# Sixteen more tokens fetch their rows of the first expert table; the high product of the one-hot gates moves to ScalarE

## What is computed

```python
def peer_ffn(xn, w_query, sub_keys, u, v):     # T = 512 tokens, H = 8 heads, K = 16 of 128 x 128 experts each
    q = (xt @ w_query).reshape(T, H, 2, PEER_HALF)
    s = jnp.einsum('thpd,hpkd->thpk', q, sub_keys)
    top_s, top_i = lax.top_k(s, K)
    cand_s = (top_s[:, :, 0, :, None] + top_s[:, :, 1, None, :]).reshape(T, H, K * K)
    cand_i = (top_i[:, :, 0, :, None] * PEER_KEYS + top_i[:, :, 1, None, :]).reshape(T, H, K * K)
    best_s, best_pos = lax.top_k(cand_s, K)
    expert_idx = jnp.take_along_axis(cand_i, best_pos, axis=-1)
    gate = jax.nn.softmax(best_s, axis=-1)
    ...
        act = jnp.einsum('td,ted->te', x_blk, u[i_blk])
        hid = jax.nn.gelu(act, approximate=False) * g_blk
        return jnp.einsum('te,ted->td', hid, v[i_blk])
```

## Time and profile before

| | us |
|---|---|
| median of 3 runs | 2528.64 (2528.29 to 2529.47) |
| the profiled execution | 2528.59 |
| its span in the trace | 2526.8 |
| PE busy | 2516.0 |
| DVE busy | 1609.6 |
| ACT busy | 1035.0 |
| POOL busy | 1001.8 |

### The profile page before, as it was taken

One profiled execution on the slowest core, in us unless ns is written; L12 is line 12 of the kernel. 1 busy time (PEld: TensorE's weight loads), 2 busy tenths in 40 slices (PEclk: granted clock), 3 DMA queues, 4 the chain that ended last, 5 costly groups with the idle time before them and its releaser, 6 DMA issues.

```text
span 2526.8 us, 35751 instructions
## 1 busy us (share of the span) xinstructions
PE 2516.0 (100%) x13652; PEld 2191.4 (87%) x13652; DVE 1609.6 (64%) x3032; ACT 1035.0 (41%) x1624; POOL 1001.8 (40%) x548
## 2 busy tenths in 40 slices
PE   9999999999999999999999999999999999999999
PEld 7789899999999988888888888888889877988888
DVE  5746989899999978888888656610216275730112
ACT  6634344444444433333333534522324365532332
POOL 3323344545555523333332044444442424254442
PEclk9999999999999999999999999999999999999999
DMA  4413255689999999999999332223322322232231
GB/s 139 142 59 119 90 156 163 216 286 372 390 397 397 327 328 339 360 349 352 354 347 342 128 117 84 92 96 97 100 93 75 125 84 74 69 117 94 99 100 59
DMA packets 193482, 488.08 MB, mean 193 GB/s; under 512 B 18560, under 2 KB 84256, under 8 KB 193056
## 3 DMA queue, kind: packets, MB, share of 16 engines
q1 hardware_dynamic: 156304, 351.49, 41.5%
q0 software_dynamic: 36864, 134.23, 14.2%
q10 hardware_dynamic: 144, 0.07, 0.0%
HBM read 442.71 MB, written 42.88 MB: 192 GB/s over the span
## 4 chain that ended last, share of the span: by engine, by line
PE 95%; ACT 1%; DVE 1%; POOL 1%; DMA 1%; issue 0%; SPq 0%; ACTq 0%; DVEq 0%; POOLq 0%
PE ps L314 30%; PE ps L316 30%; PE ps L315 30%; PE ps L1817 2%; PE ps L2838 1%; PE ps L2935 1%; PE ps L1627 1%; PE ps L2898 1%; POOL wl L303 1%; DMA wraw<-in_w_in 1%; PE ps L528 0%; ACT wh L295 0%; POOL Xl L587 0%; PE ps L2323 0%; DVE tmpb L1204 0%
## 5 line engine op out<-in xcount | busy, mean ns | idle before, releaser
L295 ACT ACTIVATE wh<-wraw 128x1024 fp32r<-128x1024 f32 x483 | 509.8, 1059 | 1178.7 <-PE ps L316 1165.3
L303 POOL TENSOR_TENSOR wl<-wraw,wh 128x1024 fp32r<-128x1024 f32 x252 | 615.0, 2447 | 929.5 <-ACT wh L295 819.2
L314 PE MATMUL ps<-Xh,wh 128*128 128x512 f32 (+2 forms) x2328 | 826.3, 355 | 2.7 <-DVE wl L1309 0.8
L316 PE MATMUL ps<-Xh,wl 128*128 128x512 f32 (+2 forms) x2328 | 814.5, 350 | 0.0
L315 PE MATMUL ps<-Xl,wh 128*128 128x512 f32 (+2 forms) x2328 | 814.4, 350 | 0.0
L314 PEld LDWEIGHTS ps<-Xh,wh 128*128 128x128 f32 x2328 | 438.4, 188 | 45.5 <-issue 6.1
L316 PEld LDWEIGHTS ps<-Xh,wl 128*128 128x128 f32 x2328 | 438.3, 188 | 38.4
L315 PEld LDWEIGHTS ps<-Xl,wh 128*128 128x128 f32 x2328 | 438.8, 188 | 36.1 <-issue 0.2
L303 DVE TENSOR_TENSOR wl<-wraw,wh 128x1024 fp32r<-128x1024 f32 x231 | 282.6, 1224 | 79.8 <-ACT wh L295 79.1
L314 PE MATMUL ps<-wh,Hh 128*128 128x512 f32 x768 | 299.0, 389 | 0.0
L316 PE MATMUL ps<-wh,Hl 128*128 128x512 f32 x768 | 298.8, 389 | 0.0
(11 more groups left out here) (336 smaller groups left out, 3012.5 us busy)
## 6 DMA issues: line engine op xcount, KB each, us to landing
wraw<-in_uT SPq DMA_DIRECT2D x128, 512.0 KB, 5.9
wraw<-in_v SPq DMA_DIRECT2D x128, 512.0 KB, 5.9
wraw<-in_up SPq DMA_DIRECT2D x128, 512.0 KB, 3.4
gA_scratch<-gl SPq DMA_DIRECT2D x122, 192.0 KB, 7.0
gl<-gA_scratch SPq DMA_DIRECT2D x122, 192.0 KB, 6.2
gG_scratch<-gbuf SPq DMA_DIRECT2D x64, 256.0 KB, 8.7
lg<-gG_scratch SPq DMA_DIRECT2D x64, 256.0 KB, 6.3
wraw<-in_w_q SPq DMA_DIRECT2D x24, 512.0 KB, 3.5
```

The lines of the kernel that those rows point to most:

```text
L295: act.activation(wh[:, n % 4, :], wraw[:, n % 4, :], ACT.Copy).then_inc(s_wh, 1)
L303: pool.tensor_tensor(wl[:, n % 4, :], wraw[:, n % 4, :], wh[:, n % 4, :].bitcast(F32), ALU.subtract).then_inc(s_wl, 1)
L314: pe.matmul(o, ah, bh, start=start, stop=False)
L316: return pe.matmul(o, al, bh, start=False, stop=stop)
```

## The change

The last NE = 16 tokens also fetch the rows of their experts in the first table. The dense layer's matmuls are 368 columns wide instead of 384, and so is gelu; for the 16 tokens `gl` is filled with ones once. Their dot products, one for each of 16 further fetches, are collected in `hid2`, go through gelu and the gate (`hE`), are turned by TensorE, cut into three bfloat16 parts and multiplied into the comparisons of the last two groups, k = 46 and 47, whose tokens take three matmuls instead of two.

Three more things are changed. The product with the high part of the gate moves for groups 0 to 45 from VectorE to ScalarE, as eight activations with a scale from `gf` for each partition, one for each token. The product with the low part comes one tile later on VectorE. In the choice of the best, ScalarE first spreads `baf` over `oh16`, so that the comparison reads two contiguous operands, and the sum over 16 is four folding additions for each half instead of one reduction.

The core of the diff:

```diff
-    oha = sb("oh", [128, 3, 4, 128, 2], F16, scope=turned)
+    oha = sb("oh", [128, 2, 4, 128, 2], F16, scope=turned)
+    xrow2 = sb("xrow2", [128, 1024], scope=turned)
...
+    FETCH, E_LAST = [], 0
+    for _k in range(SP):
+        FETCH.append(("own", _k))
+        if len(FETCH) >= 26 and len(FETCH) % 5 == 1 and sum(w == "extra" for w, _ in FETCH) < NE:
+            FETCH.append(("extra", sum(w == "extra" for w, _ in FETCH)))
+            E_LAST = len(FETCH)
     DOT = {}
-    for _k in range(SP):
-        DOT.setdefault(46 + _k * 81 // SP, []).append(_k)
+    for _n in range(SP + NE):
+        DOT.setdefault(28 + _n if _n < NE else 46 + (_n - NE) * 81 // SP, []).append(_n)
+    E_IDX, E_HID, E_GELU, E_MUL, E_TURN, E_PARTS = 46, 106, 109, 110, 111, 113
+    NGE = (ND - NE) // 8
...
         def equal(w):
-            dve.tensor_tensor(oh16[:, w, :].rearrange("p (s a) -> p s a", a=16),
-                              baf[:, w, :].unsqueeze(2).to_broadcast([128, 128, 16]),
-                              iob[:, :].unsqueeze(1).to_broadcast([128, 128, 16]), ALU.is_equal).then_inc(s_sec, 1)
+            dve.wait_ge(s_secx, 3 * tc + 1 + w)
+            o3 = oh16[:, w, :].rearrange("p (s a) -> p s a", a=16)
+            dve.tensor_tensor(o3, o3, iob[:, :].unsqueeze(1).to_broadcast([128, 128, 16]), ALU.is_equal).then_inc(s_sec, 1)
...
-        def total(w):
-            dve.tensor_reduce(slot[:, k2, w, :], oh16[:, w, :].rearrange("p (s a) -> p s a", a=16), AX.X,
+        def total(w, k):
+            o3, n = oh16[:, w, :].rearrange("p (s a) -> p s a", a=16), 8 >> k
+            out = o3[:, :, 0:n] if n > 1 else slot[:, k2, w, :].unsqueeze(2)
+            dve.tensor_tensor(out, o3[:, :, 0:n], o3[:, :, n:2 * n], ALU.add).then_inc(s_sec, 1)
...
         if j == 0:
-            pe.wait_ge(s_oh, 4 * k + 4)
+            pe.wait_ge(s_oh, 3 * k + 3 if k < NGE else 3 * NGE + 5 * (k - NGE + 1))
-        for w in range(2):
+        for w in range(1, len(hot)):
...
         for m in range(128):
-            pe_linear(pe, W_U, [m], B_U, None, lambda g: (s_gl, g + 1), t0=SP, each=each)
+            pe_linear(pe, W_U, [m], B_U, None, lambda g: (s_gl, g + 1), t0=SP, t1=T - NE, each=each)
...
             if m < 127:
                 split_hi(act, W_U + m + 4)
+            if m in EXPS:
+                act.wait_ge(s_sec, SEC_N * EXPS[m] + 53)
+                for w in range(2):
+                    act.activation(oh16[:, w, :].rearrange("p (s a) -> p s a", a=16),
+                                   baf[:, w, :].unsqueeze(2).to_broadcast([128, 128, 16]), ACT.Copy).then_inc(s_secx, 1)
...
+            if m in GATE and GATE[m] < NGE:
+                gate_high_act(act, GATE[m])
             if m in GMUL:
                 gate_copy(act, 2 * GMUL[m])
...
+            if m - 1 in GATE and GATE[m - 1] < NGE:
+                gate_low_dve(dve, GATE[m - 1])
...
+    def gate_high_act(act, k):
+        hot = oh[k % 2]
+        act.wait_ge(s_oh, 3 * k + 1)
+        for j in range(8):
+            t = 8 * k + j
+            o = act.activation(hot[1][:, j // 2, :, j % 2], hot[2][:, j // 2, :, j % 2], ACT.Copy, scale=gf[:, t:t + 1])
+        o.then_inc(s_it, 1)
+
+    def gate_low_dve(dve, k):
+        low = oh[k % 2][2]
+        dve.wait_ge(s_it, 9 + k + 1)
+        dve.tensor_tensor(low, low, of_group(gT[:, 1, :], k), ALU.mult).then_inc(s_oh, 1)
...
         for tc in range(4):
-            if tc == 3:
-                for k in range(len(fetch)):
-                    fetch_pool(pool, k)
             for h in range(8):
+                if (tc, h) == (2, 3):
+                    pool.wait_ge(s_rtp, 4)
+                    for n in range(len(fetch)):
+                        fetch_pool(pool, n)
                 pool.wait_ge(s_sec, SEC_N * tc + 2 + 6 * h)
                 split_lo(pool, W_U + SEC0 + 10 * tc + h + 4)
-        for k in range(len(fetch), SP):
-            fetch_pool(pool, k)
+                if (tc, h) > (2, 3):
+                    fetch_pool(pool, h if tc == 2 else 8 + h)
+        for n in range(16, SP + NE):
+            fetch_pool(pool, n)
```

More of the change, by code:

```diff
@@ L1801, in second_dve @@
                 dve.tensor_copy(eu[:, :], ef[:, :]).then_inc(s_idx, 1)
+            if tc == 3:
+                last = slice(96, 128)
+                dve.scalar_tensor_tensor(out=ef[last, :], in0=slot[last, 1, 0, :], scalar=128.0, in1=slot[last, 1, 1, :],
+                                         op0=ALU.mult, op1=ALU.add).then_inc(s_idx, 1)
+                dve.wait_ge(s_idx, 19)
+                dve.tensor_copy(eu[last, :], ef[last, :]).then_inc(s_idx, 1)
     s_iob = sem("s_iob")
@@ L1920, in up_dve @@
                 gate_parts_dve(dve, TURN[m - 1])
-            if m in GATE:
+            if m - 1 in GATE and GATE[m - 1] < NGE:
+                gate_low_dve(dve, GATE[m - 1])
+            if m == E_MUL:
+                dve.wait_ge(s_secx, 13)
+                dve.scalar_tensor_tensor(out=hE, in0=hE, scalar=1.0 / GSCALE, in1=gE, op0=ALU.mult,
+                                         op1=ALU.mult).then_inc(s_sec, 1)
+            if m == E_PARTS:
+                extra_parts_dve(dve)
+            if m in GATE and GATE[m] >= NGE:
+                extra_gates_dve(dve, GATE[m])
+            elif m in GATE:
                 k = GATE[m]
@@ new lines, in extra_gates_dve @@
+    def extra_gates_dve(dve, k):
+        first, second, third, equal = ohe[k % 2][0], ohe[k % 2][1], ohe[k % 2][2], ohe[k % 2][3]
+        n = 3 * NGE + 5 * (k - NGE)
+        dve.wait_ge(s_gm, 8 * (k - 1))
+        dve.wait_ge(s_dot, E_LAST)
+        dve.wait_ge(s_iob, 10)
+        for o, w in ((equal, 1), (first, 0)):
+            dve.tensor_tensor(o, iota2[:, :, :].unsqueeze(1).to_broadcast([128, 4, 128, 2]), of_group(iT[:, w, :], k),
+                              ALU.is_equal).then_inc(s_oh, 1)
+        dve.wait_ge(s_oh, n + 1)
+        for w, o in enumerate((second, third, equal)):
+            if w == 2:
+                dve.wait_ge(s_oh, n + 4)
+            dve.tensor_tensor(o, equal, of_group(gTe[:, w, :], k - NGE), ALU.mult).then_inc(s_oh, 1)
```

159 lines of the change are left out of this document (103 added, 56 removed).

## The result

| | before | after |
|---|---|---|
| median | 2529.32 us (6 runs, 2528.29 to 2529.77) | 2570.75 us (6 runs, 2569.84 to 2571.87) |
| ratio | | 1.0165, 95% interval 1.0152 to 1.0178 |
| third turn (behind tile 47) begins on TensorE | 518.29 us | 522.73 us |
| down stage begins on TensorE | 899.43 us | 942.29 us |

The changed kernel is slower by 41.4 us, and all of it arises in the up stage: the down stage begins 42.9 us later.

A forecast was written before the change was run, and what follows sets the result against it. TensorE, busy 2516.0 of 2526.8 us, was taken as the bound. Narrower matmuls -20.7, added TensorE work +1.9, the circle +48 and the choice of the best +9 make +38.2 on 2528.59: 2566.8 us, range 2535 to 2592.

The forecast's parts named there:

- narrower matmuls and the added ones: Up stage on TensorE: 368 columns save 20.7 us, tile 4.00 us; third matmul, second row turn, turn of `hE` add 1.9.
- choice of the best with early dot products: Tiles 24 to 47: VectorE and GpSimd work over the small lead makes TensorE wait 9 us, between 3 and 15.
- The circle: Tiles with gates: `split_hi`, `split_lo`, comparison, eight activations, gate copies in series; 15.96 us per three tiles against TensorE's 13.88; 48 us.
- turn of `hE`: Late tiles with gates: TensorE's added turn of the 16 tokens' values, counted as 0.1 us.
- the small DMA at the entry into the gates: Small DMAs on SP were said to lie tiles ahead of their readers and cost nothing.
- The sign that was named for it: Tiles with gates: TensorE idle before gate matmuls for the low product, about 1 us in most groups, near 48 in all.
- The first (TensorE stays the bound, 2518.8): Tiles with gates: eight activations take 1.39 us or less, so the loop is hidden; 2518.8 us, chance 0.11.
- The second, that fetches bind: Tiles with gates: full DMA engines lose 12 us of the gain over 74 shorter tiles; 2530.6 us, chance 0.04.
- The third (no overlap with float16): Tiles with gates: activations with float16 operands of step 2 don't overlap, 79 us in place of 48; 2597.8 us, chance 0.07.

The follow-up runs named there:

- e8: e3 without the 16 further fetches and their dot products, the first four GpSimd fetches again ahead of the last section (16 tokens' gate part missing); 2517.17 us.
- e6: e5 with the conversion of `iota` to `iota2` on ScalarE instead of VectorE; 2524.84 us.
- e3: Changed kernel with the same instructions, but from tile 48 VectorE does the low product and the comparisons ahead of `split_lo` instead of behind it; 2532.05 us.
- e5: e3 with the turn of `hE` one tile later (112, not 111) and `hid2` collected four tiles earlier (102, not 106); 2526.56 us.
- e2: Kernel before with only the move: high product on ScalarE as eight activations, low product one tile later on VectorE, still 384 columns; 2556.26 us.
- e10: e6 with only eight early dot products, in tiles 28 to 42, and 136 in tiles 46 to 126; `hid2` collected at tile 104; 2523.30 us.
- e11: e6 with no early dot products, all 144 in tiles 46 to 126; `hid2` collected at tile 105; 2532.80 us.

## Why the prediction was right, and where its terms were not

Forecast 2566.8, measured 2570.75, inside the range; the direction, the place and the mechanism of the main term held. The terms, with what the runs showed for each (the first is the sum of 48 x 0.16 = 7.7 saved and 0.9 for the second row turn, the second of 80 x 0.16 = 13 saved and 1.0 added):

| term | forecast | measured | from |
|---|---|---|---|
| narrower matmuls and the added ones, to the third turn | -6.8 | -7.0 | e8: 511.33 - 518.29 |
| the same behind it | -12.0 | -10.8 | e6: 370.3 - 381.1 |
| choice of the best with early dot products | 9 | 11.4 to 12.2 | e8 against after and e3 |
| the circle | 48 | 39.6 | e3 against after |
| turn of `hE` | 0.1 | 5.3 | e5 against e3 |
| the small DMA at the entry into the gates | 0 | 4.4 | e6 against e5, their profiled runs |

**Narrower matmuls: right.** 368 columns stand 0.166 us apart, as stated, and the tile takes 4.00:

```profile
600.10 0.33 PE L326 MATMUL ps<-Xl,wh 128*128 128x368 f32 x1
600.26 0.33 PE L327 MATMUL ps<-Xh,wl 128*128 128x368 f32 x1
```

**The circle: the mechanism is right, the size was 8 us too high.** The eight activations took 2.50 us, 0.30 apart, where the forecast had 2.43 and 0.29 from a row with other types. The first tile took 6.26 for 6.35, the second 5.90 for 5.98, since `split_lo` hands over after 1.13 to 1.14 and not 1.20. The third tile goes by its dot products: 1.14 + 0.60 + 1.14 each, 4.03 us with two. The 24 tiles without a group hold 1.5 on average, the forecast had 1.58, so it is 3.45 for 3.63. The sum is 15.61 in place of 15.96, and TensorE loses 1.73 per three tiles and not 2.08: 22 x 1.73, and 2 x 0.77 for the pairs (9.71 against 8.94), is 39.6, what e3 gives. That the two agree to the digit is chance, since each kernel has a wait of its own at the first groups, 3.66 us in the changed one and 2.17 in e3. The same numbers give for e2, with its tile of 4.16 and so 14.36 for three and 9.26 for two, 22 x 1.25 + 2 x 0.45 = 28.4; it measured 408.3 - 381.1 = 27.2. The sign that was named for it, TensorE idle before its gate matmuls, was to be near 48 us and is 33.0 in 33 waits, of 0.77 or 1.16 us in most groups. A part of the rest is slower work behind a wait: the 16 matmuls of such a group take 1.08 us and not 0.94. A forecast that lives on the difference of two sums, 15.96 less 13.88, takes an error of 2% in one of them as 17%.

**The choice of the best: 3 us too low, and for a part by other means.** The bounds of 3 and 15 held it. Forecast were waits of TensorE in tiles 38 to 47. They are there, but fewer: 0.51 and 0.84 at tile 37 and its turn, 2.51 at tile 38 (forecast 2), next to none in the eight tiles that were to lose 3.7, and 1.87 and 0.26 at tile 47 and its turn (forecast 3.5). In all TensorE idles 6.4 us up to the third turn. Of the other 5.0 the clock (below) is at most 3.4, and the rest wasn't followed. The duration of a tile there, 4.46 forecast from GpSimd's own two rows, was 4.36, so that GpSimd's work sets it, or nearly, was right. VectorE had no slack in it, though: the 1.15 of its dot product, taken from a place where GpSimd was idle, was 481.13 - 479.51 = 1.62 beside GpSimd's subtraction. That was missing in the working.

**The turn of `hE` and the small DMAs: the steps that failed.** "The turn of `hE` 0.1" counted TensorE's instruction and not what its bank waits for: the gate copy, which the change had queued behind eight activations. The prediction named those copies as queued there, but asked only who waits for them in the circle. Also "lie tiles ahead of their readers: nothing" failed for one small DMA, the 16 tokens' gates, whose reader is the first gate copy: 2.8 us of TensorE in e5. In the changed kernel itself nothing waits for it, as ScalarE comes to that gate copy only at 543.1.

**The clock: not forecast.** In four places the granted clock fell to 0.50, the level of 1.2 GHz, during or right behind an idle time of TensorE of 1.87 to 5.43 us. Each row is a stretch around or behind such an idle time, clock in the third column from the end:

```profile
474.00:480.00 6.00, 4.06 (x15) 4.09 (x16) 5.79 (x18) 0.19 (x1) 5.84 (x3) 0.72 0.44 149
516.00:520.00 4.00, 3.32 (x11) 3.35 (x12) 4.00 (x10) 3.60 (x6) 1.35 (x1) 0.59 0.80 251
538.00:546.00 8.00, 7.07 (x39) 7.10 (x40) 7.25 (x12) 4.72 (x12) 3.19 (x2) 0.62 0.87 320
862.00:868.00 6.00, 4.66 (x16) 4.65 (x17) 0.65 (x2) 1.20 (x3) 3.34 (x3) 0.50 0.87 295
```

6 x 0.28 + 4 x 0.41 + 8 x 0.38 + 6 x 0.50 = 9.4 us is what these rows hold, and 10.3 with the clock's edges outside of them. It is the most that it cost; a part lies in idle time. It is contained in the measured terms above. The short waits of about 1 us in front of most groups left the clock at 1.00: in e2, which has only those, its mean is 1.000.

**The rivals.** The first (TensorE stays the bound, 2518.8) was told off by the 0.30 between activations; e8, which has no early dot products either, shows that without a circle and without the 16 fetches the kernel takes 2517. The second, that fetches bind, was put down to shorter tiles and priced 12 us. e6, whose tiles are 4.00, loses nearly nothing, 370.3 against 369.1 by the forecast's own terms. With 8 and 16 fetches more e10 and e11 do lose. The third (no overlap with float16) didn't come.

So the mechanism was right by its working, but that the total is 4 us off and not more is luck, since the errors lay on both sides: -8 for the circle, against +3 for the choice of the best, +5 for the turn and +4 at the entry.

## What to carry to other kernels

Before a step moves to another engine, draw the circle of instructions that hand on to each other within one tile and add up its links; shares of busy time (ScalarE 45%) don't show it. If it is too long, look first for a reordering that takes one link out of it: 39.6 us came back without a changed instruction. And for every instruction that is queued behind a new one ask for all its readers, the reuse of its buffer or bank too. A small transfer that an old instruction newly waits for belongs to this list: one of 8 KB held TensorE up for 2.8 us.
